# A residual transposed by VectorE and a memory round trip in a streaming-encoder block, with five smaller reorderings

## The reference

```
h = rms(x, g_mix); z = h @ w_in            # split: za 512, zu 512, zv 512, zq 512, gates 3*1024
ya = gelu(s5(za)); ya = (ya * sigmoid(ya @ w_glu + b_glu)) @ w_a_out
yb = (gelu(zu) * mix(layernorm(gelu(zv)))) @ w_b_out
yc = attention(zq, rms(mem, g_mem) @ w_kv) @ w_c_out      # 4 heads, 256 memory rows
x  = x + (g0*ya + g1*yb + g2*yc) @ w_out                  # first residual: x1
hf = rms(x, g_ffn)
x  = x + (silu(hf @ w_gate) * (hf @ w_up)) @ w_down       # second residual: x1 + feed-forward
return rms(x, g_final)
```

## Time and profile before

| | us |
|---|---|
| median of 3 runs | 777.4 |
| lowest, highest | 776.43, 777.72 |
| the profiled execution | 777.84 |
| its span, first to last instruction | 776.1 |
| PE busy | 765.6 |
| DVE, ACT, POOL busy | 541.6, 354.3, 315.8 |

### The profile page before, as it was taken

The page is one execution under the profiler, slowest core; times in us unless marked ns, Lnnn a source line. Parts: engine busy times, 40 slices in busy tenths (PEclk is TensorE's granted clock), DMA queues, the critical chain, the costliest instruction groups (busy, mean ns, idle before and its releaser), DMA issues.

```text
span 776.1 us, 9751 instructions
## 1 busy us (share of the span) xinstructions
PE 765.6 (99%) x3576; PEld 630.8 (81%) x3576; DVE 541.6 (70%) x729; ACT 354.3 (46%) x526; POOL 315.8 (41%) x169
## 2 busy tenths in 40 slices
PE   9999999999999999999999999999999999999996
PEld 7778887788888888888888888888888888778885
DVE  6999997684848484345865677777776777635686
ACT  6896567644545434543433333332323233444463
POOL 4456646233333333444444344534444453920000
PEclk9999999999999999999999999999999999999999
DMA  7744332132222432232324465666756557677852
GB/s 274 297 142 135 110 109 86 31 102 82 82 82 82 132 139 82 82 108 84 106 96 146 147 206 180 214 230 203 228 186 196 204 200 246 196 246 249 280 179 109
DMA packets 39667, 121.98 MB, mean 157 GB/s; under 512 B 4048, under 2 KB 4176, under 8 KB 37840
## 3 DMA queue, kind: packets, MB, share of 16 engines
q1 hardware_dynamic: 39488, 121.26, 47.1%
q10 hardware_dynamic: 144, 0.26, 0.1%
HBM read 104.99 MB, written 16.52 MB: 157 GB/s over the span
## 4 chain that ended last, share of the span: by engine, by line
PE 78%; DVE 13%; ACT 3%; issue 2%; DMA 2%; POOL 1%; SPq 0%; POOLq 0%; DVEq 0%; ACTq 0%
PE bank L1557 21%; PE bank L1558 21%; PE bank L1559 21%; PE bank L1926 4%; PE bank L1928 4%; PE bank L1927 4%; DVE pow_tmp L969 3%; DVE tab_tmp L969 1%; DVE s5p L969 1%; PE bank L1798 1%; DMA xT<-xt_dram 1%; DMA raw<-mix_dram 1%; DVE m_lo L974 1%; ACT prob L655 1%; DVE h_lo L974 0%
## 5 line engine op out<-in xcount | busy, mean ns | idle before, releaser
L500 POOL TENSOR_TENSOR w_lo<-raw,w_hi 128x1024 fp32r<-128x1024 f32 x90 | 219.1, 2434 | 298.1 <-ACT w_hi L561 298.1
L561 ACT ACTIVATE w_hi<-raw 128x1024 fp32r<-128x1024 f32 x112 | 118.6, 1060 | 309.1 <-PE bank L1559 302.3
L1557 PE MATMUL bank<-h_hi,w_hi 128*128 128x512 f32 x608 | 238.2, 392 | 0.5 <-DVE th L969 0.4
L1559 PE MATMUL bank<-h_hi,w_lo 128*128 128x512 f32 x608 | 236.7, 389 | 0.0
L1558 PE MATMUL bank<-h_lo,w_hi 128*128 128x512 f32 x608 | 236.6, 389 | 0.0
L1557 PEld LDWEIGHTS bank<-h_hi,w_hi 128*128 128x128 f32 x608 | 114.1, 188 | 25.5 <-DVE th L969 1.3
L1559 PEld LDWEIGHTS bank<-h_hi,w_lo 128*128 128x128 f32 x608 | 114.1, 188 | 23.9
L1558 PEld LDWEIGHTS bank<-h_lo,w_hi 128*128 128x128 f32 x608 | 114.2, 188 | 23.3 <-issue 0.2
L505 POOL TENSOR_TENSOR w_lo<-raw,w_hi 128x512 fp32r<-128x512 f32 x48 | 67.2, 1422 | 56.3 <-ACT w_hi L561 49.7
L969 DVE TENSOR_TENSOR mix<-mix 128x512 f32<-128x512 f32 x44 | 47.2, 1072 | 10.5 <-DMA mix<-w_dram 9.4
L969 DVE TENSOR_TENSOR lo<-raw,hi 128x1536 fp32r<-128x1536 f32 (+1 forms) x19 | 33.3, 1757 | 28.8 <-ACT hi L888 28.8
(11 more groups left out here) (297 smaller groups left out, 1391.7 us busy)
## 6 DMA issues: line engine op xcount, KB each, us to landing
raw<-w_dram SPq DMA_DIRECT2D x112, 512.0 KB, 3.4
mix<-w_dram SPq DMA_DIRECT2D x11, 1024.0 KB, 7.7
mix_dram<-mix SPq DMA_DIRECT2D x11, 1024.0 KB, 6.4
raw<-w_dram SPq DMA_DIRECT2D x32, 256.0 KB, 3.9
raw<-mix_dram SPq DMA_DIRECT2D x28, 256.0 KB, 3.9
half_dram<-odd SPq DMA_DIRECT2D x11, 256.0 KB, 7.9
second<-half_dram SPq DMA_DIRECT2D x3, 768.0 KB, 6.0
raw<-mix_dram SPq DMA_DIRECT2D x3, 768.0 KB, 4.3
```

The source lines that it names most:

```text
L500: nc.gpsimd.tensor_tensor(w_lo[:, s, :], raw[:, s, :], fv(w_hi[:, s, :]), ALU.subtract).then_inc(w_ready, 1)
L561: nc.scalar.activation(w_hi[:, slot, :], raw[:, slot, :], ACT.Copy).then_inc(w_rounded, 1)
L1557: mm(out, a[0], b[0], start=first, stop=False)
L1559: return mm(out, a[1], b[0], start=False, stop=last)
```

## The change

1. **x1 turned by VectorE.** PE's four groups of transposes go. After the FFN norm's sums DVE does 16 block transposes (32x32 blocks, 128x256 each) of `xT` into `x1_sq`. SP stores these in 8 DMAs of 256 KB to `x1_dram` (pieces of 1 KB), and loads the whole, 2 MB in pieces of 4 KB, token-major into `y_out` in one DMA. Features are renumbered on the host (`ORDER`) so that this gives the right order. DVE adds x1 in SBUF instead of reading it with the banks.
2. **Low-part passes last** in the three behind a short one (threes 12 and 16): PE does all hi*hi and lo*hi matmuls once ACT has rounded, and waits for DVE's low part only then.
3. **Seven raw places** for the units instead of five.
4. DVE makes `mdiag` ahead of the products of `bb_tmp` and `bpow`.
5. ACT rounds tile T_VU+6 ahead of `softmax_scale(2)`. DVE does half of the last table step and both its sums later, the sums behind `vM`.
6. PE's first gate product behind the SGU waits for the third SGU bank, the second gate for the fourth.

```diff
+        x1_sq = [at(f"x1_sq{i}", o_a + ((6 + i) * PAIRS + 3) * 4 * HALF, [P, KD, KD, 32]) for i in range(2)]
-        UNIT_SLOT = (0, 1, 2, 3, 4, 0, 1, 2, 0, 1, 2)
+        raw_d = [at(f"raw_d{i}", o_h + 12288 + 4096 * i, [P, TILE]) for i in range(3)]
+        raw_e = at("raw_e", o_e + 12288, [P, TILE])
+        UNIT_SLOT = (0, 1, 2, 3, 4, 5, 6, 0, 1, 2, 6)
# SP
+            def store_x1(h):
+                sp.wait_ge(x1_turned, h + 1)
+                for i in range(4):
+                    sp.dma_start(x1_d[KD * h:KD * (h + 1), :, i, :].rearrange("j a f -> a j f"),
+                                 x1_sq[h][32 * i:32 * i + 32, :, :, :].rearrange("a j k b -> a j (k b)")
+                                 ).then_inc(x1_moved, 16)
             for t in range(T_WO, T_DN):
                 next_weights(t)
                 i, j = divmod(t - T_FF, 4)
+                if i == 1 and j < 2:
+                    store_x1(j)
+                if i == 2 and j == 0:
+                    sp.wait_ge(x1_moved, 16 * 8)
+                    sp.dma_start(y_out[:, :, :], x1_d.rearrange("(t j) a i f -> (j a) t (i f)", t=4)
+                                 ).then_inc(x1_moved, 16)
...
-                elif 3 <= k < 5:
+                elif 3 <= k < 6:
                     sp.wait_ge(w_used, T_DN)
-                elif k >= 5:
-                    unit_split(sp, {5: 0, 6: 1, 7: 2, 8: 5, 9: 6, 10: 7}[k])
+                elif k == 6:
+                    sp.wait_ge(mix_stored, 16 * PAIRS)
+                elif k > 6:
+                    unit_split(sp, {7: 0, 8: 1, 9: 2, 10: 6}[k])
...
-            for k in range(6, 10):
+            for k in range(6, PAIRS):
                 load_unit(k)
             load_three(0)
-            load_unit(10)
# ACT
             round_weights(T_VU + 5)
+            round_weights(T_VU + 6)
             softmax_scale(2)
             gelu_u(1)
-            round_weights(T_VU + 6)
             round_weights(T_VU + 7)
# DVE (token_scale(2, 2, ...) moves ahead of the bb_tmp products)
             head_scale(2)
-            table_half(NC // 2, (0, 1))
             center_v(3)
             scale_v(3)
+            table_half(NC // 2, (0,))
             scale_u(2)
             take_pt(1)
             head_max(3)
-            go(table_sum(NC // 2, 0))
-            table_sum(NC // 2, 1).then_inc(tables_ready, 1)
+            table_half(NC // 2, (1,))
             dve.wait_ge(w_used, T_VU + 7)
...
+            go(table_sum(NC // 2, 0))
+            table_sum(NC // 2, 1).then_inc(tables_ready, 1)
...
+            for h in range(2):
+                for k in range(KD):
+                    ins = V.transpose(x1_sq[h][:, :, k, :], xT[:, k, h * HALF:(h + 1) * HALF].rearrange(
+                        "p (j a) -> p j a", a=32))
+                ins.then_inc(x1_turned, 1)
             before(dve, ff_g, ff_u, ff_lo)
...
-            for u in range(2, 5):
-                low_three(u)
+            low_three(2)
+            dve.wait_ge(x1_moved, 16 * 9)
+            dve.wait_ge(s5_ready, 2)
+            go(tt(x1_two(2, 1), x1_two(2, 1), s5[:, :, :], ALU.add))
+            low_three(3)
+            go(tt(x1_two(0, 1), x1_two(0, 1), s5[:, :, :], ALU.add))
+            low_three(4)
+            dve.wait_ge(s1_ready, 2)
+            go(tt(x1_two(2, 0), x1_two(2, 0), s1[:, :, :], ALU.add))
...
-            go(tt(flat(u2[:, :, :]), flat(u2[:, :, :]), flat(s5[:, :, :]), ALU.add))
+            go(tt(x1_two(2, 1), x1_two(2, 1), u2[:, :, :], ALU.add))
             low_three(13)
             steps.wait()
             for j in range(2):
-                tt(u2[:, j, :], bank[6 + j][:, :], u2[:, j, :], ALU.add).then_inc(c_ready, 1)
-            go(tt(flat(s5[:, :, :]), flat(s5[:, :, :]), flat(u3[:, :, :]), ALU.add))
+                tt(x1_at(2 + j, 1), bank[6 + j][:, :], x1_at(2 + j, 1), ALU.add).then_inc(c_ready, 1)
+            for j in range(2):
+                tt(x1_at(j, 1), x1_at(j, 1), u3[:, j, :], ALU.add).then_inc(c_ready, 1)
             low_three(14)
-            for j in range(2):
-                tt(s5[:, j, :], bank[2 + j][:, :], s5[:, j, :], ALU.add).then_inc(c_ready, 1)
+            go(tt(x1_two(0, 0), x1_two(0, 0), u3[:, :, :], ALU.add))
             low_three(15)
# PE (turn_x1 and its calls go)
-            pe.wait_ge(sgu_taken, 4)
+            pe.wait_ge(sgu_taken, 3)
+                    elif b == 1:
+                        pe.wait_ge(sgu_taken, 4)
...
+            def behind_short(u, b, c0, k0, k1):
+                pe.wait_ge(rounded3, u + 1)
+                for k in range(k0, k1):
+                    for j in range(2):
+                        a, w = second_half(k, j, c0), three(u, k - k0)
+                        mm(bank[b + j][:, :], a[0], w[0], start=False, stop=False)
+                        mm(bank[b + j][:, :], a[1], w[0], start=False, stop=False)
+                pe.wait_ge(ready3, u + 1)
+                for k in range(k0, k1):
+                    for j in range(2):
+                        a, w = second_half(k, j, c0), three(u, k - k0)
+                        ins = mm(bank[b + j][:, :], a[0], w[1], start=False, stop=False)
+                ins.then_inc(used3, 1)
```

More of the change, by code:

```diff
@@ L70 @@
 N_SMALL = C_D + 16
+ORDER = np.arange(D).reshape(4, KD, 32).transpose(1, 0, 2).reshape(D)
 TWO_PI = 2 * np.pi
@@ L129, in build, with x1_at, x1_two @@
         y_out = at("y_out", o_x, [P, 4, D])
+        x1_sq = [at(f"x1_sq{i}", o_a + ((6 + i) * PAIRS + 3) * 4 * HALF, [P, KD, KD, 32]) for i in range(2)]
+        def x1_at(t, n):
+            return y_out[:, t, n * T:(n + 1) * T]
+        def x1_two(t, n):
+            return y_out[:, t:t + 2, n * T:(n + 1) * T]
         raw_c = at("raw_c", o_s + (4 * C_BRE + 63) // 64 * 64, [P, TILE])
-        raw_d = [at(f"raw_d{i}", o_h + 12288 + 4096 * i, [P, TILE]) for i in range(2)]
-        unit_raw = [raw[:, 0, :], raw[:, 1, :], raw_c[:, :], raw_d[0][:, :], raw_d[1][:, :]]
-        UNIT_SLOT = (0, 1, 2, 3, 4, 0, 1, 2, 0, 1, 2)
+        raw_d = [at(f"raw_d{i}", o_h + 12288 + 4096 * i, [P, TILE]) for i in range(3)]
+        raw_e = at("raw_e", o_e + 12288, [P, TILE])
+        unit_raw = [raw[:, 0, :], raw[:, 1, :], raw_c[:, :], *(r[:, :] for r in raw_d), raw_e[:, :]]
+        UNIT_SLOT = (0, 1, 2, 3, 4, 5, 6, 0, 1, 2, 6)
         UNIT_DVE = (6, 8)
@@ L284, in build @@
         mix_loaded, mixed, mix_stored, half_stored = sems("mix_loaded mixed mix_stored half_stored")
-        unit_loaded = [sem(f"unit_loaded{i}") for i in range(5)]
+        unit_loaded = [sem(f"unit_loaded{i}") for i in range(7)]
         unit_half, unit_dve, p5_done, s1_ready, s5_ready = sems("unit_half unit_dve p5_done s1_ready s5_ready")
@@ L1098, in _ @@
                 low_tile(norms["m"], m_hi, m_lo, memf, C_GMEM, k)
+            token_scale(2, 2, mtstd[:, :], mtrstd[:, :], mdiag[:, :, :], diag_m)
             bre, bim, cre, cim = (grid(c0) for c0 in (C_BRE, C_BIM, C_CRE, C_CIM))
@@ L1111, in _ @@
             link(tt(bpow[1][:, L - 1, :, :], bb_tmp[:, 2, :, :], bb_tmp[:, 3, :, :], ALU.add))
-            token_scale(2, 2, mtstd[:, :], mtrstd[:, :], mdiag[:, :, :], diag_m)
             def times(to, of, a_re, a_im, conj, n):
@@ L1529, in _ @@
                     dve.wait_ge(p2_done, 1)
-                tt(s1[:, j, :], bank[4 + j][:, :], s1[:, j, :], ALU.add).then_inc(c_ready, 1)
+                tt(x1_at(2 + j, 0), bank[4 + j][:, :], x1_at(2 + j, 0), ALU.add).then_inc(c_ready, 1)
             low_three(16)
@@ L1541, in _ @@
             for t in range(2):
-                tt(x2g[:, t, :], s5[:, t, :], g_row[:, T:D], ALU.mult).then_inc(x2g_ready, 1)
+                tt(x2g[:, t, :], x1_at(t, 1), g_row[:, T:D], ALU.mult).then_inc(x2g_ready, 1)
+            steps.wait()
             for j in range(2):
                 dve.wait_ge(dn_done, j + 1)
-                tt(u3[:, j, :], bank[j][:, :], u3[:, j, :], ALU.add).then_inc(c_ready, 1)
+                tt(x1_at(j, 0), bank[j][:, :], x1_at(j, 0), ALU.add).then_inc(c_ready, 1)
             scaled(2, 0)
@@ L1909, in _ @@
             feed(0, 1, ff_u)
-            def turn_x1(t, n, alone=False):
-                for j in range(4):
-                    ins = mm(bank[OUT_BANK[t][n]][:, j * P:(j + 1) * P], xT[:, 4 * n + j, t * P:(t + 1) * P], ident,
-                             start=j == 0, stop=alone and j == 3, is_transpose=True)
-                return ins
             pe.wait_ge(norms["f"]["std"], 1)
@@ L1991, in _ @@
                     for j in range(2):
[L1992 removed]
+                        ins = step(4 + j, second_half(k, j, HALF), three(u, k - k0), k == 0, k == PAIRS - 1)
                         if k == PAIRS - 1 and j == 0:
@@ L2009, in _ @@
                         for j in range(2):
-                            ins = step(j, second_half(k, j, 0), three(u, k - k0), False, False)
+                            ins = step(j, second_half(k, j, 0), three(u, k - k0), k == 0, False)
                     ins.then_inc(used3, 1)
@@ L2118 @@
```

(3 more changed lines are left out.)

49 lines of the change are left out of this document (19 added, 30 removed).

## The result

| us | before | after |
|---|---|---|
| median | 777.01 (4 runs) | 772.23 (4 runs) |
| lowest, highest | 776.43, 777.72 | 771.45, 773.15 |
| the profiled execution, its span | 777.84, 776.1 | 771.45, 769.7 |

The ratio is 0.9937, with a 95% interval of 0.9921 to 0.9953: 4.8 us less. The forecast for the median was 771.9. Timed once more, with five runs beside nine of before, it took 772.24 against 777.93, ratio 0.9924 (0.991 to 0.9937), 5.7 us less.

A forecast was written before the change was run, and what follows sets the result against it. PE, busy 99% of the span, was taken as the bound. Gains of 1.5 + 0.8 + 0.8 + 0.3 + 0.45 + 1.1 + 0.55 = 5.5 us took the profiled 777.84 to 772.3; the median, 0.44 lower, to 771.9, range 770.3 to 775.3.

The forecast's parts named there:

- the rival in which early gains are taken back: Before 140 us, DVE or ACT, close behind PE, take back 2.1 us of the gains: 774.0 us, chance 0.16.
- Units 9 and 10: With seven raw places PE's late starts at units 9 and 10 go: 1.5 us gained, bounds 0.3 and 1.6.
- Three 0: Removing the transposes inside three 0, where PE stays slower than ACT and DVE, gains 0.8 us, bounds 0 and 0.9.
- Turns ahead of three 11 and behind 12: Two transpose groups go, but PE waits for DVE's low part at three 13: 0.8 of 1.58 us stays.
- Ahead of three 15: This transpose group goes, but PE waits for three 17's low part: 0.3 of 0.79 us stays.
- mdiag: DVE makes mdiag over 2 us earlier, closing PE's hole there: 0.45 us gained, bounds 0 and 0.7.
- T_VU+6: Earlier rounding by ACT closes PE's holes ahead of and inside this tile: 1.1 us gained, bounds 0.4 and 1.3.
- SGU: PE's wait for the fourth bank before the first gate product goes: 0.55 us gained, bounds 0.3 and 0.7.
- The transposes: 16 DVE transposes at 0.333 us take 5.3 us under 6.4 of cover before PE's up product: cost 0.
- The rival of whole durations: Each DVE transpose waits for the one before to end: 6.7 us against 6.4 of cover, 772.3 us, chance 0.04.
- DMAs: 4 MB more traffic, including the 2 MB load, costs 0, by ACT's slack of 4.4 us.
- The slower rival: DVE transposes take 0.68 us each and are shut out once: PE's up product held 6.9 us, 778.8 us, chance 0.03.

The follow-up runs named there:

- e7: The kernel before with only the seven raw places for the units added: 776.13 us, ratio 0.9974 to before.
- e4: The changed kernel with DVE's low parts of threes 13 and 17 moved ahead of other DVE work: 771.78 us, ratio 0.9919 to before.
- e5: e4 with DVE's low part of three 14 also moved ahead of the two x1 sums: 770.28 us, ratio 0.9895 to before.
- e9: The changed kernel with mdiag made behind the products of bb_tmp and bpow again: 772.32 us, ratio 0.9937 to before.
- e11: The changed kernel with PE's first gate product waiting for the fourth SGU bank again: 771.58 us, ratio 0.9926 to before.
- e10: The changed kernel with T_VU+6 rounded behind softmax_scale(2) and gelu_u(1), and DVE's last table step as before: 773.46 us, ratio 0.9951 to before.
- e12: The changed kernel with 8 more DVE transposes, into a place nothing reads, ahead of the 16: 773.28 us, ratio 0.9947 to before.
- e6: The changed kernel with 16 more DVE transposes, into a place nothing reads, ahead of the norm's drains: 777.69 us, ratio 0.9992 to before.
- e8: The changed kernel with two more 2 MB memory-to-memory copies issued behind the 2 MB load: 786.23 us, ratio 1.0106 to before.

## Why the prediction was right

The forecast was 771.9 in a range of 770.3 to 775.3; measured were 772.23 and 772.24. The sum was 5.5 us; the two comparisons gave 4.8 and 5.7, the distances 6.2. The waits and places were right in all terms but one, the SGU. That the total is so close is partly luck: the terms were short by 0.7 us against the distances, and the times show less than the distances.

Why they do is only partly shown. The intervals of the two comparisons reach from 3.7 to 6.1 and from 4.9 to 7.0 us, so the timing hardly tells them from 6.2. Without its edit the hole at `mdiag` costs 0.26 in one profile (e7) and not 0.59, and PE gives back some 0.1 at 61 us. That is a small part of the rival in which early gains are taken back, and one of the prediction's own signs of being wrong, a new wait between 47 and 140 us. PE's arrival at `mdiag` was 47.38 in the one profile of before; in the ten with the edit it lies at 47.1 in the middle, 0.3 earlier, but they spread over 1.7.

- **Units 9 and 10, 1.5.** By the distance 1.76: the two holes with their restarts are 1.6, and 0.1 lay at the start of three 0. Starts 2.8 apart were forecast, 2.72 measured. Alone (e7) the time fell by 2.1, though its one profile has other holes in the units.
- **Three 0, 0.8.** 1.82 less the 0.79 of the turn ahead of three 11 is 1.03: the 0.82 of the turn, and two gaps of 0.31 instead of 0.23 that before had behind the start of three 0 and behind the group. The last 0.05 is not explained.
- **Turns ahead of three 11 and behind 12: 0.8 of 1.58 stays.** PE waits 0.76 at three 13, and starts it 0.92 late (0.8 was forecast). The chain named in the prediction (low part 12, bank sums, the u2 sum, low part 13) is the one in the rows, and e4 and e5 showed it by moving it. "Just in time for three 14" was right to a hair: in e4 the same sums, pushed behind, stopped three 14 for 0.99.
- **Ahead of three 15: 0.3 of 0.79 stays.** The wait at three 17 is 0.47, and it starts 0.63 late (0.5 was forecast). Of 2.37 removed in these two terms 2.37 - 0.92 - 0.63 = 0.82 would be left; by the distances it is 0.79 + 0.27 = 1.06, as forecast (1.1), because before had a longer gap of 0.31 behind each of the three groups as well, 0.08 more than the regular one. (The other longer gaps behind three 11, 0.3 in all in either kernel, cancel.) Between the two terms it came out a little otherwise than forecast.
- **mdiag, 0.45.** 0.59 by the distance, and e9 loses 0.53 of it again; 0.26 in e7's profile, and some 0.1 goes back at 61 us. The "0.42 idle" of the profile was too small by the 0.16 that the matmul in front is drawn past its successor's regular start.
- **T_VU+6, 1.1.** 1.03 (e10).
- **SGU, 0.55.** The size is 0.7, but the step named the wrong cause. The term was costed as the fourth bank's wait, with edit 5 at zero here. Edit 5 already brings the fourth bank in time (e11), by the rows through ACT, which comes to `o_hiT` earlier; the wait of PE on three banks adds nothing to it. Either gives the whole, so two such terms must not be added; the sum came out right because it gave edit 5 nothing at this place.
- **The transposes, 0.** 0.333 each from the four 128x256 operations was exact (5.33 for 16), and so was the cover: "1 us left" is 1.0 in e12 and 1.05 in e6. The rival of whole durations (6.7 us) is out. The Trainium skill's page VectorE: DVE Perf Modes (The DRAIN you can't avoid) has the next operation wait for an empty pipe. If that wait is taken to last as long as the operation is drawn, 0.42 us, the trace differs: it has 0.333. By the Trainium skill's page VectorE: DVE Perf Modes (The three transpose paths) I had estimated 0.44 each, 7.1 in all and a hold of 0.7; the trace has 0.333 and no hold.
- **DMAs, 0.** The 4.38 of ACT's slack is unchanged, and e8 shows what stands behind it.
- **The slower rival, 778.8,** was priced too low where it would have come true. Its hold of 6.9 us was counted as 6.9. e6 shows that after a hold of 4.28 PE loses 1.6 more at half the clock, e8 2.8 after 11.5.

The gate was forecast 2.1 us earlier: it is 2.8 and 2.3 by the two starts that were profiled (139.81 and 140.33 against 142.59). Of this 0.3 comes from the first gate matmul being drawn while the value products drain: by the second gate matmul (140.45 and 140.97 against 142.93) it is 2.5 and 2.0.

## What to carry to other kernels

Once PE is full, a step taken off it is worth only what the next supplier leaves: some 1.5 us of the 3.2 that the transposes took went back because two low parts on DVE came late, and ordering DVE's work by when PE needs it (e5) brought 1.8 us more than the change had. Two edits that relieve the same wait are worth it once, so undo each alone before adding up. And cost work that is moved under a cover by its start-to-start time, then give the cover's remainder beside it, since here it was 1.0 us for 16 operations.

## What the runs showed of the hardware

- **A long hold costs more than its length.** In e6 PE had 3.7 us without a matmul. It restarted at full clock, and 1.6 us later the granted clock was down to 0.50 (the window from 433.3 to 436.6 us), with starts 0.43 us apart, which is 1.2 GHz in place of 2.4; it cost 1.6 us on top of the hold. After 11.3 us (e8) 13 matmuls ran so, and it cost 2.8 us. After 1.1 us (e12) the starts behind the restart stayed 0.23 apart. The Trainium skill's page TensorE: Matmul & The Clock Gate (Part 1: The HAM clock gate) says that an idle array goes back to 1.2 GHz; the traces of e6 and e8 agree (0.50, and 0.50 from 477 to 480). Before and after show nothing of it between the first microseconds and the last product.
- **DVE transposes of 128x256 fp32** start 0.333 us apart, as a sum or product of that shape does, 16 or 32 in a row alike (5.33 and 5.30 us per 16).
- **Two more 2 MB copies from memory to memory** behind a 2 MB load delayed a 512 KB load behind them until ACT had waited 17.58 us for it.
